# Eight more expert blocks computed densely, with half of the dense first-table work moved beside the making of the gates

## What is computed

```
q  = x @ w_query                         # 8 heads, two halves of 128 each
s1, s2 = q1 @ sub_keys_1, q2 @ sub_keys_2          # 128 first keys, 128 second keys
i1, i2 = top 16 of s1, top 16 of s2
idx    = i1 * 128 + i2 of the best 16 of the 256 sums      # of 16384 experts
gates  = softmax(best 16 sums)
hid    = gelu(sum_d expert_u[idx, d] * x[d]) * gates
out    = sum over 8 heads x 16 slots of hid * expert_v[idx]
```

## Time and profile before

| | us |
|---|---|
| median of three runs | 3005.09 |
| lowest and highest | 3003.09, 3007.17 |
| the profiled execution | 3004.93 |
| its span, first to last instruction | 3002.9 |

### The profile page before, as it was taken

One profiled execution on the slowest core, in us unless ns is written; L12 is line 12 of the kernel. 1 busy time (PEld: TensorE's weight loads), 2 busy tenths in 40 slices (PEclk: granted clock), 3 DMA queues, 4 the chain that ended last, 5 costly groups with the idle time before them and its releaser, 6 DMA issues.

```text
span 3002.9 us, 45413 instructions
## 1 busy us (share of the span) xinstructions
PE 2736.4 (91%) x17100; PEld 2038.3 (68%) x17100; DVE 1923.8 (64%) x3184; ACT 1178.5 (39%) x2298; POOL 668.0 (22%) x568
## 2 busy tenths in 40 slices
PE   8999999999999998999999999999976678888884
PEld 7886788888888887989999889777753322222220
DVE  6888566555656565455445558987769875555555
ACT  1003443334333344425334444645456642222232
POOL 0000000000000000040000002544448765454453
PEclk9999999999999998999999999999977779999886
DMA  6333545555555553443555657999999999999997
GB/s 244 140 141 111 206 157 185 187 191 183 194 182 193 184 192 122 155 152 141 182 182 182 248 199 250 372 418 408 415 375 408 397 409 417 409 420 391 411 409 300
DMA packets 131297, 785.51 MB, mean 262 GB/s; under 512 B 34630, under 2 KB 34630, under 8 KB 35846
## 3 DMA queue, kind: packets, MB, share of 16 engines
q1 hardware_dynamic: 55424, 393.68, 35.5%
q0 software_dynamic: 75712, 389.74, 32.3%
HBM read 940.23 MB, written 4.19 MB: 315 GB/s over the span
## 4 chain that ended last, share of the span: by engine, by line
PE 57%; DMA 20%; DVE 12%; issue 6%; ACT 3%; POOL 1%; DVEq 1%; POOLq 0%; SPq 0%; ACTq 0%
DMA s_u<-in_expert_u,s_u_index 17%; PE bank L1847 10%; PE bank L1841 10%; PE bank L1843 10%; PE bank L1842 10%; PE bank L1848 5%; PE bank L1937 4%; DVE s_u L1706 4%; PE bank L2240 4%; PE bank L2292 2%; DMA s_v<-in_expert_v,s_v_index 2%; DVE s_cacc L1217 2%; ACT s_spread L1050 2%; DVE s_w_lo L1128 1%; DVE s_yrow L1390 1%
## 5 line engine op out<-in xcount | busy, mean ns | idle before, releaser
L1128 DVE TENSOR_TENSOR s_w_lo<-s_raw,s_w_hi 128x2048 fp32r<-128x2048 f32 x258 | 592.6, 2297 | 577.8 <-ACT s_w_hi L628 577.4
L628 ACT ACTIVATE s_w_hi<-s_raw 128x2048 fp32r<-128x2048 f32 x256 | 490.5, 1916 | 750.9 <-PE bank L1843 475.4
L1847 PE MATMUL bank<-s_a,s_w_hi 128*128 128x512 f32 x1408 | 494.7, 394 | 3.2 <-DVE s_w_lo L1128 3.2
L2292 PE MATMUL bank<-s_v,s_spread 128*32 128x512 f32 x2048 | 302.8, 721 | 183.1 <-ACT s_spread L1050 115.9
L1706 DVE CUSTOM_DVE_ANT_0 s_u<-s_u,s_xn_late 128x1024 f32<-128x1024 f32 x256 | 303.8, 1224 | 246.8 <-DMA s_u<-in_expert_u,s_u_index 246.5
L1050 ACT ACTIVATE s_spread<-s_ident,s_hid 32x32 f32<-32x32 f32 x1024 | 325.6, 318 | 205.5 <-DVE s_hid L1756 188.0
L1848 PE MATMUL bank<-s_a,s_w_lo 128*128 128x256 f32 x1408 | 395.1, 281 | 0.0
L585 POOL DMA_INDIRECT s_u<-in_expert_u,s_u_index x256 | 300.0, 1172 | 416.4 <-DVE s_halfdot L1706 240.4
L601 POOL DMA_INDIRECT s_v<-in_expert_v,s_v_index x256 | 317.9, 1242 | 196.8 <-PE bank L2292 115.5
L1706 DVE CUSTOM_DVE_ANT_0 s_u<-s_u,s_xn 128x1024 f32<-128x1024 f32 x256 | 303.8, 1224 | 60.3 <-DMA s_u<-in_expert_u,s_u_index 59.3
L1841 PE MATMUL bank<-s_a,s_w_hi 128*128 128x256 f32 x1152 | 325.1, 282 | 3.4 <-DVE s_a L1152 1.8
(11 more groups left out here) (321 smaller groups left out, 3809.8 us busy)
## 6 DMA issues: line engine op xcount, KB each, us to landing
s_raw<-in_stream SPq DMA_DIRECT2D x292, 1024.0 KB, 4.7
s_raw<-in_expert_v SPq DMA_DIRECT2D x40, 1024.0 KB, 8.9
s_raw<-in_dense_u SPq DMA_DIRECT2D x37, 1024.0 KB, 8.7
s_u<-in_expert_u,s_u_index POOLq DMA_INDIRECT x256, 17.4
s_v<-in_expert_v,s_v_index POOLq DMA_INDIRECT x256, 17.6
s_panel_early<-in_dense_u POOLq DMA_DIRECT2D x3, 1024.0 KB, 11.5
s_xres<-in_x SPq DMA_DIRECT2D x2, 1024.0 KB, 6.0
out<-s_out_row SPq DMA_DIRECT2D x32, 64.0 KB, 3.3
```

Source lines behind the costliest of these rows:

```text
L628: act.activation(w_hi[s % 2][:, :], raw[s][:, :], ACT.Copy).then_inc(hi_ready, 1)
L1128: dve.tensor_tensor(w_lo[s % 2][:, :], raw[s][:, :], w_hi[s % 2][:, :].bitcast(f32), ALU.subtract)\
L1847: pe.matmul(dst, left[0], both, start=start, stop=False)
L2292: ins = pe.matmul(bank[4 * t + q][c * Q:(c + 1) * Q, :], spread[g % NW][:, q, :], v_slot[k % NV][:, c * 512:(c + 1) * 512], start=False, s ...
```

## The change

- DENSE goes from 40 to 48: gathers skip the rows of 48 first keys, and there are 48 panels of each table. `ha` grows by 8 KB a partition, and eight of its 48 blocks lie apart (`ha_apart`), in the place that the seventh second-table row had. So NV goes from 7 to 6.
- Of the 48 first-table panels the first 28 pass in iterations 0 to 16. The last 20 pass in iterations 17 to 29, one or two in each, beside the gates. They use banks 4 and 5 only, since 6 and 7 hold gates.
- Gates of tokens that come before their panel are copied into `ha` by DVE instead of multiplied. When the panel has passed, ACT writes gelu for those tokens into a small buffer of two (`late_act`) and for the others straight into `ha`, and DVE multiplies the buffer into `ha` two rounds after the panel's iteration (`landed`).
- Second-table panels: 16 in every nine iterations from 34 to 60 instead of three in every two.
- The order of the dense blocks changes with this (`dense_block`), and the key rows are 48 wide instead of 40.

```diff
-DENSE = 40
+DENSE = 48
+FIRST_U, LATE_U, APART = 28, 20, 8
@@ u_panels_in
-    return range(6 + 34 * (i - 2) // 15, 6 + 34 * (i - 1) // 15) if i < 17 else range(0)
+    if i < 17:
+        return range(6 + (FIRST_U - 6) * (i - 2) // 15, 6 + (FIRST_U - 6) * (i - 1) // 15)
+    return range(FIRST_U + LATE_U * (i - 17) // 13, FIRST_U + LATE_U * (i - 16) // 13) if i < 30 else range(0)
+def u_bank(d):
+    if d < FIRST_U:
+        return 4 + d % 4, d // 4
+    return 4 + (d - FIRST_U) % 2, FIRST_U // 4 + (d - FIRST_U) // 2
+def gated_before(g):
+    fours = 8 * (g - 18) if g < 20 else 4 * (g - 16)
+    return max(0, min(fours, T // 4) // 2 - 2)
+LANDS_IN = {d: i + 2 for i in range(30) for d in u_panels_in(i) if d >= FIRST_U}
@@ v_panels_in
-    return range(3 * (i - 34) // 2, min(DENSE, 3 * (i - 33) // 2)) if i >= 34 and 3 * (i - 34) // 2 < DENSE else range(0)
+    return range(16 * (i - 34) // 9, 16 * (i - 33) // 9) if 34 <= i < 61 else range(0)
@@ places
-    NU, NV, NW, NH, BATCH, LAG = 5, 7, 4, 4, 4, 4
+    NU, NV, NW, NH, BATCH, LAG = 5, 6, 4, 4, 4, 4
-    ha = place("s_ha", [128, DENSE, T], S + 24 * K)
+    ha_main = place("s_ha", [128, DENSE - APART, T], S + 24 * K)
+    ha_apart = place("s_ha_apart", [128, APART, T], ring0 - 16 * K)
+    late_act = place("s_late_act", [128, 2, T], pick_at)
@@ ACT, dense_hidden
-                act.activation(ha[:, dense_block(d), :], bank[b][:, 0:T], ACT.Gelu_apprx_tanh).then_inc(bank_empty[b], 1)
+                done = 0
+                if late >= 0:
+                    done = GATE_TOKENS * gated_before(LANDS_IN[d])
+                    if late == 0:
+                        act.wait_ge(expert_ready, TT * PH)
+                    wait(act, late_landed, late - 1)
+                    act.activation(late_act[:, late % 2, 0:done], bank[b][:, 0:done], ACT.Gelu_apprx_tanh)
+                act.activation(ha_rows(dense_block(d), slice(done, T)), bank[b][:, done:T], ACT.Gelu_apprx_tanh).then_inc(bank_empty[b], 1)
@@ DVE, gated
-                some = ha[:, :, GATE_TOKENS * group:GATE_TOKENS * (group + 1)]
-                dve.tensor_tensor(some, some, bank[b][:, 0:GATE_TOKENS * DENSE].rearrange("p (t g) -> p g t", t=GATE_TOKENS), ALU.mult)\
-                    .then_inc(bank_empty[b], 1)
+                for first, last, rows in ((0, APART, ha_apart), (APART, DENSE, ha_main)):
+                    put = min(max(missing, first), last)
+                    if put > first:
+                        ins = dve.tensor_copy(rows[:, 0:put - first, tokens], gates[:, first:put, :])
+                    if put < last:
+                        some = rows[:, put - first:, tokens]
+                        ins = dve.tensor_tensor(some, some, gates[:, put:last, :], ALU.mult)
+                ins.then_inc(bank_empty[b], 1)
+            def landed(d):
+                late, (b, k) = d - FIRST_U, u_bank(d)
+                groups = gated_before(LANDS_IN[d])
+                for group in (groups - 2, groups - 1):
+                    gates_taken = n.after(f"empty{6 + group % 2}", FIRST_U // 4 + 2 + group // 2)
+                    dve.wait_ge(bank_empty[6 + group % 2], gates_taken)
+                dve.wait_ge(bank_empty[b], n.after(f"empty{b}", k + 1))
+                some = ha_rows(dense_block(d), slice(0, GATE_TOKENS * groups))
+                dve.tensor_tensor(some, some, late_act[:, late % 2, 0:GATE_TOKENS * groups], ALU.mult).then_inc(late_landed, 1)
@@ DVE, the rounds
+                    for d in range(FIRST_U, DENSE):
+                        if turn == 0 and LANDS_IN[d] == g:
+                            landed(d)
```

More of the change, by code:

```diff
@@ L129, in dense_block @@
 def dense_block(d):
-    return d + 16 if d < 24 else d - 16 if d < 32 else d - 32
+    return (d + 4) % FIRST_U + LATE_U if d < FIRST_U else DENSE - 1 - d
 def score_row(th):
@@ L442, in two_layers @@
         spread_ready, v_used = sem("spread_ready"), sem("v_used")
+        late_landed = sem("late_landed")
         acc_done, out_ready, stored = sem("acc_done"), sem("out_ready"), sem("stored")
@@ L609, in _ @@
                     gather_u(k)
-                for first in {4: (2, 3), 5: (4, 5), 6: (6,)}.get(k, ()):
+                for first in {4: (2, 3), 5: (4, 5)}.get(k, ()):
                     gather_v(first)
@@ L1054, in dense_hidden @@
             def dense_hidden(d):
-                b = 4 + d % 4
+                b, late = u_bank(d)[0], d - FIRST_U
                 act.wait_ge(panel_used, NPANELS + 1 + d + 1)
-                if d == 32:
-                    act.wait_ge(expert_ready, PH)
-                act.activation(ha[:, dense_block(d), :], bank[b][:, 0:T], ACT.Gelu_apprx_tanh).then_inc(bank_empty[b], 1)
+                done = 0
[6 more added lines that the diff above has]
+                act.activation(ha_rows(dense_block(d), slice(done, T)), bank[b][:, done:T], ACT.Gelu_apprx_tanh).then_inc(bank_empty[b], 1)
             def slots_transposed(t):
@@ L1082, in one_keys @@
                 act.activation(four, four, ACT.Relu, scale=-1.0, bias=1.0).then_inc(one_key_ready, 1)
-            slots_stored = [n.after(f"empty{6 + t}", DENSE // 4 + 1) for t in range(TT)]
+            slots_stored = [n.after(f"empty{6 + t}", FIRST_U // 4 + 1) for t in range(TT)]
             for g in range(ROUTES * GROUPS):
@@ L1723, in one_keys_2 @@
                     for t in range(TT):
-                        dve.wait_ge(bank_empty[6 + t], n.after(f"empty{6 + t}", DENSE // 4 + 1))
+                        dve.wait_ge(bank_empty[6 + t], n.after(f"empty{6 + t}", FIRST_U // 4 + 1))
                 wait(dve, one_key_used, 2 * (m - 2))
@@ L1739, in one_keys_late, with gated @@
                                   iota_f[:, :].unsqueeze(1).to_broadcast([128, 8, NKEYS]), keys_2, ALU.is_equal).then_inc(one_key_late_ready, 1)
-            def gated(group):
+            def gated(group, missing):
                 b = 6 + group % 2
@@ L1745, in gated @@
                     for a in range(2):
-                        dve.wait_ge(bank_empty[4 + a], n.after(f"empty{4 + a}", DENSE // 4))
+                        dve.wait_ge(bank_empty[4 + a], n.after(f"empty{4 + a}", FIRST_U // 4))
                 dve.wait_ge(one_key_used, GATE_TOKENS // 4 * (group + 1))
-                some = ha[:, :, GATE_TOKENS * group:GATE_TOKENS * (group + 1)]
-                dve.tensor_tensor(some, some, bank[b][:, 0:GATE_TOKENS * DENSE].rearrange("p (t g) -> p g t", t=GATE_TOKENS), ALU.mult)\
-                    .then_inc(bank_empty[b], 1)
+                if group == 0:
+                    dve.wait_ge(res_taken, 1)
+                tokens = slice(GATE_TOKENS * group, GATE_TOKENS * (group + 1))
+                gates = bank[b][:, 0:GATE_TOKENS * DENSE].rearrange("p (t g) -> p g t", t=GATE_TOKENS)
+                for first, last, rows in ((0, APART, ha_apart), (APART, DENSE, ha_main)):
[15 more added lines that the diff above has]
+                dve.tensor_tensor(some, some, late_act[:, late % 2, 0:GATE_TOKENS * groups], ALU.mult).then_inc(late_landed, 1)
             def hidden(g):
@@ L1806, in _ @@
                         route(route_in(g), turn)
-                    fours = token_fours_in(g)
+                    for d in range(FIRST_U, DENSE):
+                        if turn == 0 and LANDS_IN[d] == g:
+                            landed(d)
+                    fours, missing = token_fours_in(g), sum(LANDS_IN[d] > g for d in range(FIRST_U, DENSE))
                     for f in fours[turn * len(fours) // 4:(turn + 1) * len(fours) // 4]:
                         if f >= 4 and f % 2 == 0:
-                            gated(f // 2 - 2)
+                            gated(f // 2 - 2, missing)
                         if f % 2 == 0:
@@ L1815, in _ @@
                     if g == 32 and turn < 2:
-                        gated(T // GATE_TOKENS - 2 + turn)
+                        gated(T // GATE_TOKENS - 2 + turn, 0)
                 dots_summed(g)
@@ L2228, in dense_u_panel @@
             def dense_u_panel(d):
-                b = 4 + d % 4
+                b, k = u_bank(d)
                 if d == 0:
                     pe.wait_ge(xnt_ready, 1)
-                into(b, d // 4)
+                into(b, k)
                 if d < NE:
@@ L2249, in dense_v_panel @@
                         for c in range(4):
-                            ins = pe.matmul(bank[4 * t + q][c * Q:(c + 1) * Q, :], ha[:, d, t * 128 + q * Q:t * 128 + (q + 1) * Q],
+                            ins = pe.matmul(bank[4 * t + q][c * Q:(c + 1) * Q, :], ha_rows(d, slice(t * 128 + q * Q, t * 128 + (q + 1) * Q)),
                                             raw[r][:, c * 512:(c + 1) * 512], start=False, stop=d == DENSE - 1 and t == 0)
@@ L2258, in slots_transposed @@
                 pe.wait_ge(gates_ready, PH * (t + 1))
-                into(6 + t, DENSE // 4)
+                into(6 + t, FIRST_U // 4)
                 for kind in range(3):
@@ L2267, in token_four @@
                 if f % 2 == 0:
```

(6 more changed lines are left out.)

8 lines of the change are left out of this document (4 added, 4 removed).

## The result

The changed kernel takes 3031.25 us (3028.71 to 3036.06, six runs) against 3004.53 us for the kernel before (six runs): a ratio of 1.009, 95% interval 1.0079 to 1.0102. It is slower by 26.7 us, outside the predicted range of 2980 to 3024 us. The profiled execution took 3031.06 us, its span 3029.0.

The account below looks back on a forecast made before the run. DMA was taken as full nearly everywhere, with PE and VectorE also bounding stretches. Terms -28 - 4 + 3 + 45 - 6 - 11 - 4 = -5 us gave 3000.0 us, range 2980 to 3024.

Parts of the forecast that it names:

- A: Rounds 2 to 16, 34 first-table panels become 22: 294 us to 266, -28, with VectorE's 261 us as the floor.
- G: Rounds 20 to 30, gates plus sixteen late panels: gapless PE work of 190.6 us and a 7.4 us tail, +45.
- Rival 1: PE keeps gaps in the gates' rounds 20 to 30, waiting for spreads; with half the waits 3020 us; chance 0.22.
- V: Rounds 34 to 60, second-table panels 40 to 48: DMA 468 to 473 us at 410 GB/s; taken as 471, -11.
- PE's nearness: Rounds 34 to 60: PE's 455 us of work stands 3% from DMA's bound, taken to cost nothing.
- six places: Rounds 34 to 60: each second-table row place must cycle in 26 us, landing takes 19.4; fits narrowly.
- Rival 3: Six places starve rounds 34 to 60, which stay at 490 us: 3019 in all, or 3011 at 482; chance 0.12.
- T: Rounds 17 to 19, where gates begin: +3 from late panels on PE's path; round 17, half a panel less, gives 4.
- H: Rounds 31 to 33: DMA ahead with places full, 37 us for 43, -6 (range -8 to 0).
- E: Rounds 61 to 63 and the end: three rounds with 0.53 MB less each, -4.
- Rival 2: DMA is all that counts, so 17 MB net give their whole 41 us: 2964, partly true 2980; DMA-like chance 0.18.
- The clock: Rounds 20 to 30: with panels filling PE's gaps, its clock rises from 0.73 to the full 2.4 GHz level.

Follow-up runs that it names:

- e2: Changed kernel with 36 first-table panels first and 12 late instead of 28 and 20: 3012.3 us, 1.0024 to the kernel before.
- e15: Changed kernel with 32 panels first and 16 late, seven places up to the gates and from round 34, second-table panels spread to round 63: 3002.32 us, 0.999.
- e13: Kernel before with a fixed even pattern of skipped rows, 68.75% of the rows kept: 2959.81 us, 0.9848.
- e11: Changed kernel with rows skipped in a fixed even pattern by partition and slot, 62.5% kept: 2983.7 us, 0.9925.
- e5: Changed kernel with 47 of its 48 second-table panels multiplied with only half of the tokens, all panels still loaded: 3031.16 us.
- e1: Kernel before with six places for second-table rows instead of seven: 3011.73 us, 1.002.
- e4: Changed kernel with a seventh place for second-table rows from round 34 on: 3032.04 us, 1.0087.
- e6: Changed kernel with only half of each second-table panel loaded, all multiplications kept: 2979.07 us.
- e14: Changed kernel with 36 panels first and 12 late, seven places up to the gates and from round 34, second-table panels spread to round 63: 3004.87 us, 0.9993.
- e7: Changed kernel with seven places for second-table rows up to the gates and from round 34 on, six between: 3027.31 us, 1.0068.
- e10: Kernel before with the bounds check of both gathers at 80 first keys instead of 88, so eight first keys' rows are not fetched: 2963.51 us.
- e12: Changed kernel with the bounds check above the table, so that every row is fetched: 3355.4 us.
- e9: Changed kernel with a sixth place for first-table rows from round 34 on: 3040.33 us, 1.0114.

## Why the prediction was wrong

- *A, VectorE takes over as the bound*: right. Most route rounds after take 20.1 us, the floor was 261 us, 268.5 was measured for the 266 taken. PE was busy 84% of it (225 us), not below 80%.
- *G, PE's floor of 190.6 us and a tail of 7.4*: right, in size and mechanism; +46 for +45, gapless, clock 0.97. Rival 1 didn't come. e2 and e15 show it from the other side, and also that DMA stands right below PE's floor: with six and three panels fewer G took 178 and 181.5 us at 394 and 396 GB/s, PE busy 160.5 and 173.6.
- *V, "DMA: ... 468 to 473 us at 410"*: this step failed. The mechanism (DMA sets V) and the bytes were right; the rate was carried over as if it belonged to the chip, while it belonged to how evenly the rows fell. In this kernel the rows kept after the change were fewer and less even: 398 GB/s. That is 14 of the 31 us. With even rows the same step gives what was forecast, 466 to 454 us (e13, e11). I gave PE's nearness and six places as the risks; neither was one (e5, e1, e4). PE's floor of 455 us was itself too high, as e6's 431 shows. Rival 3 comes nearest for V (482 to 490 us), with a cause that isn't there, and its 3019 us, like rival 1's 3020, are still 11 to 12 us short of the time.
- *T, +3 and -4 for round 17*: this step failed too, by 10 us. The +3 held: from the first gates to the end of the last ones of T it took 37 us before and 40 after. The -4 didn't: from the start of T to the first gates it took 31 us before and 36 after. In the chain of the profile after, 21.7 us of these are one first-table gather from issue to landing; in e11 it is 12.8, the first gates come after 29 us, and T is 68 in all, as in e13. So the greater part of the 10 us comes with the uneven rows, as far as these profiles show it. PE's work has a share too: four late panels pass in iterations 17 to 19, and T is 65.5 us with three (e15) and 64 with two (e2, e14). No run tested the shares alone. The seventh place was not it (e7).
- *H*: -3 for -6, and -3 with even rows too (e13, e11); why isn't settled. *E*: right.
- *Rival 2, all 41 us of the bytes*: wrong twice over, by the floors named against it and by the rate.
- The clock: G ran at 0.97 with PE busy throughout, against 0.73 with a third idle, and V in e5 fell to 0.82 with PE busy 69%, while its time hardly changed. This agrees with what the prediction cites from the Trainium skill (TensorE: Matmul & The Clock Gate, Part 1).

In the sum, A and G together were forecast at +17 us and came to +21; T, H, V and E were to give 22 back and cost 5 instead. G could collect nothing of the 41 us that the net bytes were worth, since PE sets it, and A only down to VectorE's floor; of the stretches that were left to DMA, the longest, V, ran at a lower rate. Each term was within 14 us of its forecast, but the sum was a small difference of large terms and came out on the other side of zero.

## What to carry to other kernels

A DMA rate read from a trace is that of its own mix of transfers. When a change alters which rows a gather skips, work out the load of the fullest engine, not of the mean: here, skipping more rows wherever they fell saved less than its bytes (19 us for 35 in e10). And when work is moved into a stretch with idle time, add it up against every engine's floor there, the transfers' too; TensorE was idle for 49 us of G and was asked for 114 (16 panels of 7.1). Where an input can be made even, as in e11 and e13, run both kernels with it: only the pair showed that the uneven rows were not what made the change slower.

## What the hardware showed

- In V, gathered rows and panels together moved at 422 to 426 GB/s when all partitions carried the same (e11, e12, e13), and at 397 to 410 when rows were skipped as they fell (e10, before, after). The DMA share is 0.99 to 1.02 in all of these and hardly tells them apart; the 40 slices of the DMA view do, by their dips (down to 313 after, none below 417 in e11).
- Nearly half of the panel products in V taken away changed V by 2 us (e5), though PE had been busy 435 of 485 us.
- A sixth place for first-table rows in V gained nothing: 3040 against 3031 us, with overlapping intervals (e9).
